# A two-block transformer on one core: gates and branches token-major, six chunks on [high | low] columns, the input on its own queue

## The reference, cut to what matters

```python
def mixer(h, w_in, b_f, conv_w, w_branch, w_out):
    proj = jnp.einsum("bsd,dn->bsn", h, w_in)
    q, k, v, f_logit, g_b, g_c, hc, gate_conv, gate_attn = jnp.split(proj, _SPLITS, axis=-1)
    ya = g_b * causal_depthwise_conv(g_c * hc, conv_w)
    ...
    yb = forgetting_attention(q.reshape(shp), k.reshape(shp), v.reshape(shp), logf)
    ya_d = jnp.einsum("bsc,cd->bsd", ya, w_branch[0])
    yb_d = jnp.einsum("bsc,cd->bsd", yb, w_branch[1])
    merged = jax.nn.sigmoid(gate_conv) * ya_d + jax.nn.sigmoid(gate_attn) * yb_d
    return jnp.einsum("bsd,de->bse", merged, w_out)

def first_block(x, ...):
    h = rmsnorm(x, norm_mix_pre[l])
    x = x + rmsnorm(mixer(h, ...), norm_mix_post[l])
    h = rmsnorm(x, norm_ffn_pre[l])
    x = x + rmsnorm(swiglu(h, w_gate_up[l], w_down[l]), norm_ffn_post[l])
```

## Time and profile before

| what | value |
|---|---|
| median of 3 runs | 983.38 us |
| profiled execution | 984.04 us, span 982.2 us |
| TensorE clock granted | 0.997 |
| busy: PE, DVE, ACT, POOL | 970.5 (99%), 678.4 (69%), 497.7 (51%), 16.7 us (2%) |
| DMA | 176.25 MB, 179 GB/s over the span |
| chain that ended last | PE 94%, DVE 2%, ACT 1%, DMA 1%, issue 1% |
| time in the changed part | GB starts at 50.25 us, the first output chunk at 166.99 |

### The profile page before, as it was taken

One profiled execution on the slowest core, in us unless ns is written; L12 is line 12 of the kernel. 1 busy time (PEld: TensorE's weight loads), 2 busy tenths in 40 slices (PEclk: granted clock), 3 DMA queues, 4 the chain that ended last, 5 costly groups with the idle time before them and its releaser, 6 DMA issues.

```text
span 982.2 us, 14216 instructions
## 1 busy us (share of the span) xinstructions
PE 970.5 (99%) x5692; PEld 856.6 (87%) x5692; DVE 678.4 (69%) x697; ACT 497.7 (51%) x666; POOL 16.7 (2%) x20
## 2 busy tenths in 40 slices
PE   8999999999999999999999999999999999999997
PEld 8999999888888888888888888899988888888885
DVE  5657867757777777876767776576664677777776
ACT  6354565773343434834344346574966554343433
POOL 0000000022000000000000000000000000000000
PEclk9999999999999999999999999999999999999998
DMA  7955374654555555555555554635444445656551
GB/s 236 278 173 172 129 279 130 230 179 142 202 194 198 189 187 212 172 173 199 188 184 188 187 207 132 221 120 171 138 163 150 147 153 171 214 171 214 171 171 43
DMA packets 124358, 176.25 MB, mean 179 GB/s; under 512 B 4042, under 2 KB 98460, under 8 KB 124188
## 3 DMA queue, kind: packets, MB, share of 16 engines
q1 hardware_dynamic: 123596, 173.23, 53.0%
q10 hardware_dynamic: 720, 2.43, 0.7%
HBM read 174.60 MB, written 1.05 MB: 179 GB/s over the span
## 4 chain that ended last, share of the span: by engine, by line
PE 94%; DVE 2%; ACT 1%; DMA 1%; issue 1%; SPq 0%; DVEq 0%; ACTq 0%
PE up_banks L579 12%; PE gate_banks L579 12%; PE bank L426 9%; PE bank L427 9%; PE bank L428 9%; PE up_banks L426 9%; PE up_banks L428 8%; PE up_banks L427 8%; PE up_banks L584 6%; PE gate_banks L584 6%; DMA stage<-in_w_in 1%; PE bank L513 1%; DVE w_lo L1506 1%; PE bank L530 1%; PE bank L721 0%
## 5 line engine op out<-in xcount | busy, mean ns | idle before, releaser
L1512 DVE TENSOR_TENSOR w_lo<-stage,w_hi 128x2048 fp32r<-128x2048 f32 x81 | 185.5, 2290 | 96.6 <-ACT w_hi L1009 96.6
L1506 DVE TENSOR_TENSOR w_lo<-stage,w_hi 128x2048 fp32r<-128x2048 f32 x79 | 180.9, 2294 | 84.7 <-ACT w_hi L1002 84.5
L1002 ACT ACTIVATE w_hi<-stage 128x2048 fp32r<-128x2048 f32 x79 | 150.9, 1913 | 74.7 <-PE up_banks L428 39.0
L1009 ACT ACTIVATE w_hi<-stage 128x2048 fp32r<-128x2048 f32 x81 | 152.8, 1905 | 0.0
L579 PE MATMUL gate_banks<-act_both,w_hi 128*128 128x512 f32 x528 | 135.5, 393 | 0.5 <-DVE act_both L1519 0.5
L579 PE MATMUL up_banks<-act_both,w_hi 128*128 128x512 f32 x528 | 131.7, 391 | 0.0
L426 PE MATMUL up_banks<-act_both,w_hi 128*128 128x256 f32 x416 | 119.3, 287 | 1.9 <-DVE w_lo L1506 1.4
L427 PE MATMUL up_banks<-act_both,w_hi 128*128 128x256 f32 x416 | 117.7, 283 | 0.0
L428 PE MATMUL up_banks<-act_both,w_lo 128*128 128x256 f32 x416 | 117.6, 283 | 0.0
L579 PEld LDWEIGHTS up_banks<-act_both,w_hi 128*128 128x128 f32 x528 | 96.6, 188 | 18.4
L579 PEld LDWEIGHTS gate_banks<-act_both,w_hi 128*128 128x128 f32 x528 | 93.8, 189 | 16.5 <-DVE act_both L1519 0.7
(11 more groups left out here) (339 smaller groups left out, 1488.6 us busy)
## 6 DMA issues: line engine op xcount, KB each, us to landing
stage<-in_ffn_w SPq DMA_DIRECT2D x66, 1024.0 KB, 5.3
stage<-in_w_in SPq DMA_DIRECT2D x33, 1024.0 KB, 5.3
stage<-in_w_gate_up SPq DMA_DIRECT2D x22, 1024.0 KB, 5.1
stage<-in_w_down SPq DMA_DIRECT2D x11, 1024.0 KB, 4.9
stage<-in_w_out SPq DMA_DIRECT2D x8, 1024.0 KB, 5.1
stage<-in_mem_w_kv SPq DMA_DIRECT2D x8, 1024.0 KB, 5.1
stage<-in_w_branch SPq DMA_DIRECT2D x4, 1024.0 KB, 5.2
stage<-in_mem_w_q SPq DMA_DIRECT2D x4, 1024.0 KB, 5.2
```

What stands on the lines that cost most here:

```text
L1002: act.activation(w_hi[:, place, :], stage[:, place, :], copy).then_inc(hi_done, 1)
L1009: act.activation(w_hi[:, place, :], stage[:, place, :], copy).then_inc(hi_done, 1)
L1506: dve.tensor_tensor(w_lo[:, place, :], stage[:, place, :], w_hi[:, place, :].bitcast(F32), ALU.subtract).then_inc(lo_done, 1)
L1512: dve.tensor_tensor(w_lo[:, place, :], stage[:, place, :], w_hi[:, place, :].bitcast(F32), ALU.subtract).then_inc(lo_done, 1)
```

## The change

- Gates and branches are made token-major (`up_tok`, a new `branch`); ACT reads the gates and applies the factor. `gate_c` and `gate_a` hold 2 token tiles x 1024. The branch chunks alternate convolution and attention for the first 512 columns, then for the others.
- The merged sum is turned by 16 new transposes (`turn_merged`), half ahead of branch 3, half behind the first output chunk, and ACT and DVE split it from PSUM. The memory is turned half ahead of the first output chunk, half behind the second, into other banks.
- GB to HC+1 (`BLOCKS`) multiply by [high | low] columns (`up_blocks`), block m into bank m; `scaled` reduces each bank and multiplies once. POOL waits for that multiply.
- The four pieces of x are issued by ACT, behind two small loads; SP starts with the weights.
- `lo(129)` is done in two halves with `gained` for blocks 4 to 7 between.

```diff
-BY_ACT = {V, V + 1, *range(MEMK, MEMK + 4), ...
+BY_ACT = {V, V + 1, *range(GATE_C, BR0), *range(MEMK, MEMK + 4), ...
+BLOCKS = [*range(GB, GATE_C)]
...
+        for key, b in [((c, 0), 0), ((c, 1), 1)] if c in BLOCKS else [(c, (first + i) % 2)]:
+            BEFORE[key] = next((x for x in reversed(BANK) if BANK[x] == b), None)
...
             for half, done in enumerate((half_landed, landed[0])):
-                cols = slice(512 * half, 512 * half + 512)
-                for t in range(2):
-                    sp.dma_start(x_n[:, t, cols], a["x"][0, t * P:t * P + P, cols]).then_inc(x_landed[half], 16)
...
+            for p in range(4):
+                token_pair(GATE_C + 2 * p, w_in, 3080 + 512 * p)
             for i in range(4):
-                rows(BR0 + i, a["w_branch"][0, i // 2], 0, 4, 512 * (i % 2), 512, slot(BR0 + i))
+                rows(BR0 + i, a["w_branch"][0, i % 2], 0, 4, 512 * (i // 2), 512, slot(BR0 + i))
...
+            def up_blocks(c):
+                pe.wait_ge(lo_done, c + 1)
...
+                for m in range(2):
+                    before = BEFORE[(c, m)]
+                    if isinstance(before, tuple):
+                        pe.wait_ge(up_free, FREED[before])
+                    else:
+                        wait_read(pe, before)
+                    ms = slice(m * P, m * P + P)
+                    for k in range(KD):
+                        pe.matmul(bank[UP + m], wh[:, k, ms], act_both[:, k, :, :].rearrange("p s t -> p (s t)"),
+                                  start=k == 0, stop=False, skip_group_check=True)
+                    for k in range(KD):
+                        mm = pe.matmul(bank[UP + m][:, T:2 * T], wl[:, k, ms], act_hi[:, k, :], start=False, stop=k == KD - 1,
+                                       skip_group_check=True)
+                    if m == 0:
+                        mm.then_inc(block_done, 1)
+                mm.then_inc(used, 1)
...
+            branch(0)
+            branch(1)
+            branch(2)
+            wait_read(pe, GATE_A + 3)
+            turn_merged(0)
+            branch(3)
+            pe.wait_ge(mem_landed, 16)
+            turn_memory(0)
+            turn_memory(1)
             for j in range(4):
                 pe.wait_ge(act_lo_done, 8 + 2 * j + 2)
...
+                if j == 0:
+                    turn_merged(1)
+                if j == 1:
+                    pe.wait_ge(act_lo_done, 16)
+                    turn_memory(2)
+                    turn_memory(3)
...
             act.dma_start(first_rows[:, :], ...
+            for half in range(2):
+                cols = slice(512 * half, 512 * half + 512)
+                for t in range(2):
+                    act.dma_start(x_n[:, t, cols], a["x"][0, t * P:t * P + P, cols]).then_inc(x_landed[half], 16)
...
+            gate_in(GATE_C, 0, 0)
             exps(1, L1, T)
+            gate_in(GATE_C, 0, 1)
...
+            for b in range(4):
+                merged_hi(b)
+            hi(25)
             hi(26)
...
             for b in range(KD):
+                if b == 4:
+                    for i in range(4, KD):
+                        merged_hi(i)
                 act.wait_ge(memt_turned, b // 2 + 1)
...
             def scaled(c, to, r):
+                if c not in BLOCKS:
+                    dve.tensor_tensor(to, result(c), over(r), ALU.mult).then_inc(up_free, 1)
+                    return
+                for m in range(2):
+                    if m == 0:
+                        dve.wait_ge(block_done, BLOCKS.index(c) + 1)
+                    else:
+                        dve.wait_ge(used, c + 1)
+                    dve.tensor_reduce(to[:, m, :], bank[UP + m].rearrange("p (s t) -> p t s", s=2), AX, ALU.add
+                                      ).then_inc(up_free, 1)
+                wait_read(dve, c)
+                dve.tensor_tensor(to, to, over(r), ALU.mult).then_inc(scaled_done, 1)
...
+            merge(0)
+            lo(23)
+            merge(1)
+            lo(24)
+            merge(2)
+            merged_lo(0)
+            merge(3)
             lo(25)
             lo(26)
             for b in range(KD):
+                if b == 4:
+                    merged_lo(1)
...
-            lo(129)
+            dve.wait_ge(hi_done, 130)
+            part = slice(0, CH // 2)
+            dve.tensor_tensor(w_lo[:, 129 % RING, part], ...
             gained(par, G_FFN2, 6, range(4, KD))
+            part = slice(CH // 2, CH)
+            dve.tensor_tensor(w_lo[:, 129 % RING, part], ...
+                              ).then_inc(lo_done, 1)
```

More of the change, by code:

```diff
@@ L43 @@
 BANK, BEFORE, FREED, AFTER_FFN = {}, {}, {}, {}
-BY_ACT = {V, V + 1, *range(MEMK, MEMK + 4), MEMV[0], MEMV[0] + 1, MEMV[1], MEMV[1] + 1, DQ, DQ + 1, DK, DK + 1, RV, RV + 1,
+BY_ACT = {V, V + 1, *range(GATE_C, BR0), *range(MEMK, MEMK + 4), MEMV[0], MEMV[0] + 1, MEMV[1], MEMV[1] + 1, DQ, DQ + 1, DK, DK + 1, RV, RV + 1,
           DV, DV + 1, *range(MEMQ, MEMQ + 4)}
-TOKEN_PAIRS = [V, MEMK, MEMK + 2, MEMV[0], MEMV[1], DK, DV, RV, MEMQ, MEMQ + 2]
+TOKEN_PAIRS = [V, *range(GATE_C, BR0, 2), MEMK, MEMK + 2, MEMV[0], MEMV[1], DK, DV, RV, MEMQ, MEMQ + 2]
+BLOCKS = [*range(GB, GATE_C)]
 def through_banks(chunks, first=0):
     for i, c in enumerate(chunks):
[L55 to L58, removed]
+        for key, b in [((c, 0), 0), ((c, 1), 1)] if c in BLOCKS else [(c, (first + i) % 2)]:
+            BEFORE[key] = next((x for x in reversed(BANK) if BANK[x] == b), None)
+            BANK[key] = b
+            FREED[key] = sum((x in BY_ACT) == (key in BY_ACT) for x in BANK)
 through_banks(range(Q, BR0))
@@ L156, in build @@
         y_T = k_flat[:, 1040:1040 + 2 * T].rearrange("p (a t) -> p a t", a=2)
-        gate_c, gate_a = gate[:, 0:8, :], gate[:, 8:16, :]
+        gate_c, gate_a = (gate[:, 8 * i:8 * i + 8, :].rearrange("p a b -> p (a b)").rearrange("p (t d) -> p t d", t=2)
+                          for i in range(2))
         g_s, silu, u_s, h_T = (gate[:, 2 * i:2 * i + 2, :] for i in range(4))
@@ L1796, in _, with merge @@
             lo(21)
-            scaled(GATE_A + 3, gate[:, 14:16, :], rs)
             lo(22)
-            for j in range(2):
-                dve.wait_ge(used, BR0 + j + 1)
+            def merge(j):
+                cols = slice(512 * (j // 2), 512 * (j // 2) + 512)
                 dve.wait_ge(gates_done, 2 * j + 2)
-                for i in range(2):
-                    g = gate_c[:, 4 * j + 2 * i:4 * j + 2 * i + 2, :]
-                    ins = dve.tensor_tensor(g, pair[ACC + 2 * j + i], g, ALU.mult)
-                ins.then_inc(br_free, 1)
-                lo(23 + j)
@@ new lines, in merged_lo @@
+            def merged_lo(h):
+                for b in range(4 * h, 4 * h + 4):
+                    dve.wait_ge(act_hi_done, 8 + b // 2 * 2 + 2)
+                    dve.tensor_tensor(act_lo[:, b, :], pair[UP + b // 2 % 2][:, b % 2, :], act_hi[:, b, :].bitcast(F32),
+                                      ALU.subtract).then_inc(act_lo_done, 1)
+            merge(0)
[5 more added lines that the diff above has]
+            merge(3)
```

141 lines of the change are left out of this document (79 added, 62 removed).

## The result

The changed kernel takes **988.64 us** (median of 5 runs, 988.56 to 989.05) against 983.81 for the kernel before in the same comparison (983.1 to 983.87): a ratio of 1.0053, 95% interval 1.0042 to 1.0064. It is 4.8 us slower. The forecast was 982.6, with a range up to 984.4. The nearest of the forecast's cases is the third rival, 986.8, which had a chance of 0.08; what came is 1.8 above that too.

A forecast was written before the change was run, and what follows sets the result against it. TensorE, busy 99% of the span, was taken as the bound. Terms -0.9 (start), +0.4 (stream, V wait and tail) and -0.3 (split conversion) sum to -0.8 us, from 983.38 to 982.6; range 980.0 to 984.4.

The forecast's parts named there:

- third rival: Start: x on the second queue is served behind the weights, second half landing at 14.0; 986.8 us, chance 0.08.
- Part 2: Start: x on ACT's queue lets Q+1's weights issue and land earlier; 0.9 us gained, bounds 0 to 1.8.
- the strict reading: Start: spreading loads over issuing engines gains nothing, +0.9 against the forecast, 983.5 us; as a rival, chance 0.12.
- Part 1: TensorE's stream: longer matmuls save 3.8 in gates and branches, 1.3 in six chunks; new transposes cost 1.7; net 3.4 less.
- Trainium skill's 2.5 ns a matmul: TensorE's stream: matmuls cost only their columns, stream grows 0.7 instead of shrinking 3.4; 986.7 us, rival's chance 0.01.
- Part 3: Behind V: TensorE stands 1.3 us in GB for ACT's read of V; reductions of 0.69 us covered between the six chunks.
- Part 4: Attention block's tail: the later memory turns delay an ACT and DVE chain; about 2.5 us stand, 3.4 saved become 0.4 lost.
- first rival: Tail has unseen slack, squares not holding hi(28) up, so the 3.4 saved stay; 980.1 us, chance 0.21.
- Part 5: Last FFN: splitting lo(129) removes TensorE's wait of 0.5, with 0.1 to 0.2 coming back at diag; gain 0.3 us.

The follow-up runs named there:

- no_idle_between: Changed kernel without the 12 idle matmul calls between the turns of x's two halves; 988.50 us.
- small_on_sp: Changed kernel with x as ACT's first act and the two small loads at the head of SP's queue; 983.63 us.
- before_new_start: Kernel before, only its first loads reordered: x as ACT's first act, the two small loads heading SP's queue, weights behind; 982.64 us.
- x_on_sp: Changed kernel with x back on the SP queue in the old order, all else as changed; 984.56 us.
- all_edits: Changed kernel with the load order of small_on_sp and the four edits that sp_all_reduce adds to x_on_sp; 980.37 us.
- sp_all_reduce: x_on_sp with V's second tile read before hi(8), memory squares early, lo(129) whole, first block's first reduction ahead of lo(8); 981.28 us.
- sp_squares: x_on_sp with ACT's four squares of the memory moved ahead of its wait for GATE_A; 982.73 us.
- x_first_on_act: Changed kernel with ACT issuing x ahead of the two small loads, at 0.72 us; 990.41 us.
- before_x_act: Kernel before with x's four loads moved to ACT, behind the two small ones, nothing else changed; 987.79 us.

## Why the prediction was wrong

- **Part 2 is the step that failed**, in the sentence "A transfer on ACT's queue beside the same traffic landed in 3.4 us, so that queue is not starved." The row was read as a property of the queue. It was one of place: that load was issued at 0.74, level with SP's first. x goes out from 1.91 on, behind SP's weights, and none of it moved before 5 us. From the same view I could have seen the other side, that Q+1 in the kernel before, issued at 3.83, took 10.19 us, that is, it waited its turn. I bounded the term at 0 to 1.8 us gained, although the rival held the loss: the term's bounds should have included it. Measured: +3.7, not -0.9. The term's own mechanism did occur: Q+1, issued at 1.77, landed 10.8 us later, near 12.6 and not 14.02, but TensorE no longer waited for it. The rival had the right place, x behind the weights. That its size (+3.3, from a second half at 14.0; it was turned at 14.69) came near was luck: no_idle_between shows that the second half had landed by 11.57. TensorE came to it late because it had stood for the first half and then worked slowly through the 24 idle matmuls, which the rival did not have: 1.7 us of the loss were slow matmuls.
- The gain of 0.9 itself was there to be had: with x issued first on its own queue, stretch 1 is 35.28 (small_on_sp) and 34.58 (before_new_start) against 36.22, and the kernel before gains 1.0 us (982.64). Its ratio reaches up to 1.0000, but the same order of loads is worth as much in two other pairs: 983.63 against 984.56 (small_on_sp, x_on_sp) and 980.37 against 981.28 (all_edits, sp_all_reduce). The Trainium skill, "DMA: Bandwidth & Descriptors", section "Rules for kernel authors", by which spreading issues saves only issue time, was right in that the rate at full load stayed (353 GB/s from 6 to 8 us and 377 from 8 to 10 in small_on_sp, 378 in the earlier trace rows); by the strict reading, no gain, it was not, for Q+1 went out at 2.58 and not at 3.83 and the dip was filled (335 GB/s from 4 to 5 us against 166 in the earlier trace rows).
- **Part 1, -3.4.** Steps of 0.2275 came as forecast. From GATE_C to the first turn of the memory it is 90.57 to 165.33 before and 94.45 to 166.65 after, 2.56 less; forecast 3.8 less 0.85, 2.95. Part of the 0.4 that is missing is seen: the first matmul of a product behind transposes takes some 0.1 more (a step of 0.32 and not 0.23 at 161.07, and of 0.20 and not 0.12 with 256 columns, at 108.73 in the kernel before), and the changed stretch has two such long steps more, at 108.20 and 161.07. The rest stays open. The six chunks saved 0.9, not 1.3 (40.32 to 40.53, with 1.09 of standing in it). By the Trainium skill's 2.5 ns a matmul ("TensorE: Matmul & The Clock Gate", section "Wait — 56ns, not 53.3ns?") the stream would have grown; it did not.
- **Part 3, +1.3.** Right: ACT read V at 57.18, TensorE stood 1.1 us. No wait at the other five, so a reduction, 0.69 us as forecast, beside 2.8 us of product is covered.
- **Part 4, +0.4.** Right in mechanism and order; from the start of GB to MEMK's second half it is 145.75 before and 146.49 after, +0.74. The third turn of the memory came 0.7 later than forecast because the stream saved less, and the chain behind it ran 0.4 shorter than summed (21.03 us against 21.4). The first rival (slack in the tail) falls for this kernel; but its condition, squares that do not hold hi(28) up, could be had by moving 2.4 us of squares (sp_squares).
- **Part 5, -0.3.** The sign was wrong: +0.21 to +0.3. The old wait of 0.5 is gone, as said; but the second half of lo(129) pushed mean, deviation and hi(130) by 0.25, and TensorE stood the longer for diag (0.24 at 801.04, none before) and for ffn_lo (0.42 at 813.33; before, that matmul came 1.04 us after the eight ahead of it began, now 1.53). I called the delay small at diag and did not follow it to the next wait.
- Part 4, which has 1 and 3 in it, and Part 5 were forecast at +0.1 together; x_on_sp, which is the change without Part 2, measured +1.0: 0.34 of it in Part 4 and 0.5 to 0.6 in Part 5.

Two readings of the prediction were slips that changed nothing: the waits read from the earlier trace rows leave out one of 1.0 us, ahead of the very first idle matmul, and 982.6 + 0.9 + 1.4 is 984.9, not 984.8. The range missed because its lower end was bought with the slack of the tail (0.21) and its upper end left out the rival that named the right place.

## What to carry to other kernels

A row on one queue showed here how a transfer fares from its place in the order of issue across all queues, not what its queue can do: before a load is moved, list what every queue will have issued by then. Do so for the small loads too, if the first instruction of the engine that reads the critical load needs them: in x_first_on_act 64 KB behind x cost 1.8 us. An engine's saving is worth only what the next chain leaves of it, so two waits that stand in one another's shadow, as in the six chunks, are best taken away together, and each followed to the next one.

## What the hardware showed that I had not expected

- Transfers queued by SP from 0.73 us on kept all 16 engines from x, issued at 1.91 on ACT's queue, until 5 us: 0.85 MB against 0.07, all of it other loads, in the stretch 2 to 5 us. Issued at the same time the two shared (x 0.26 MB, the weights 0.45, in x_first_on_act), and with x 0.9 us ahead of the weights x had the greater part (0.59 against 0.25, in small_on_sp).
- 64 KB landed in 3.3 us at the head of ACT's queue beside SP's weights, in 6.8 issued at 3.77 behind 1 MB of x and SP's weights, and in 1.9 with SP quiet.
- After TensorE had stood for 3.1 us, eight turns took 1.97 us and not 1.09, and the next 24 matmuls 4.12 and not 2.84. In before_x_act, where it stood for 4.2 us and the 24 took 4.41, the granted clock reads 0.50 (1.2 GHz) from 9 to 13 us; in the profile of the change it reads 1.00 at the same steps, so the steps are the surer sign. Filling the standing with idle matmuls gave 1.09 and 2.84 again.
